# A four-layer hybrid decoder step on one core: turning and gating a head's output one block at a time between parts of the next head

## The reference

```python
out   = inner @ v + (q @ state) * cross_decay        # inner: masked q k^T
state = decay * state + (k * k_decay)^T @ v
# after the last chunk, per token and head:
o = (o - mu) * rsqrt(var + LN_EPS) * gn_g            # retention
o = o * rsqrt(mean(o * o) + LN_EPS) * rms_g          # GLA
y = (silu(g) * o) @ w_out
```

## Time and profile before

| | |
|---|---|
| median of 3 runs | 4918.33 us (4916.63 to 4928.33) |
| the profiled execution: its time | 4917.5 us |
| the profiled execution: its span | 4915.8 us |
| TensorE, VectorE, ScalarE busy | 95%, 66%, 45% of the span |
| mean granted TensorE clock | 0.967 |
| retention's recurrence | 1327.4 to 1468.2 us |
| GLA's recurrence | 2690.5 to 2777.2 us |

### The profile page before, as it was taken

One profiled execution on the slowest core, in us unless ns is written; L12 is line 12 of the kernel. 1 busy time (PEld: TensorE's weight loads), 2 busy tenths in 40 slices (PEclk: granted clock), 3 DMA queues, 4 the chain that ended last, 5 costly groups with the idle time before them and its releaser, 6 DMA issues. The chain is left out here.

```text
span 4915.8 us, 114294 instructions
## 1 busy us (share of the span) xinstructions
PE 4672.5 (95%) x49481; PEld 3647.5 (74%) x49481; DVE 3222.5 (66%) x6336; ACT 2203.9 (45%) x3067; POOL 739.9 (15%) x354
## 2 busy tenths in 40 slices
PE   7999999999969999999995799999999999999998
PEld 4677789995527777799964467778997667778997
DVE  3695778546355967686445487677845488677844
ACT  3675343444215763434442277433343377433343
POOL 0462000004002630000010056000001056000000
PEclk9999999999989999999997799999999899999999
DMA  3344444444363444444441344444444344444443
GB/s 121 120 162 159 146 151 145 156 164 162 135 234 118 168 159 147 153 146 152 160 144 32 105 144 159 155 148 150 147 160 139 111 140 159 156 148 150 147 160 125
DMA packets 286871, 717.26 MB, mean 146 GB/s; under 512 B 25795, under 2 KB 103444, under 8 KB 285348
## 3 DMA queue, kind: packets, MB, share of 16 engines
q1 hardware_dynamic: 286374, 709.95, 43.7%
HBM read 679.19 MB, written 30.67 MB: 144 GB/s over the span
## 5 line engine op out<-in xcount | busy, mean ns | idle before, releaser
L1698 DVE SCALAR_TENSOR_TENSOR b_lo<-raw,b_hi 128x1024 f16<-128x1024 f32 x800 | 980.1, 1225 | 894.3 <-ACT b_hi L1507 889.0
L1507 ACT ACTIVATE b_hi<-raw 128x1024 f16<-128x1024 f32 x800 | 842.9, 1054 | 1028.4 <-PE ps L1620 1028.4
L1599 PE MATMUL ps<-x_hi,b_hi 128*128 128x320 f16 x4608 | 1272.8, 300 | 23.9 <-DVE x_lo L253 23.6
L1600 PE MATMUL ps<-x_lo,b_hi 128*128 128x320 f16 x4608 | 1273.4, 300 | 0.0
L1617 PE MATMUL ps<-w_hi,b_lo 128*128 128x256 f16 x4096 | 1118.2, 273 | 0.0
L1617 PE MATMUL ps<-w_lo,b_hi 128*128 128x256 f16 x4096 | 1118.0, 273 | 0.0
L1617 PE MATMUL ps<-w_hi,b_hi 128*128 128x256 f16 x4096 | 1117.7, 273 | 0.0
L1620 PE MATMUL ps<-w_lo,b_hi 128*128 128x64 f16 x4096 | 789.3, 193 | 0.0
L1620 PE MATMUL ps<-w_hi,b_lo 128*128 128x64 f16 x4096 | 789.3, 193 | 0.0
L1620 PE MATMUL ps<-w_hi,b_hi 128*128 128x64 f16 x4096 | 789.0, 193 | 0.0
L1587 POOL TENSOR_TENSOR b_lo<-raw,b_hi 128x1024 f16<-128x1024 f32 x288 | 616.5, 2141 | 852.8 <-ACT b_hi L1505 852.8
(11 more groups left out here) (282 smaller groups left out, 6910.8 us busy)
## 6 DMA issues: line engine op xcount, KB each, us to landing
raw<-in_peer_uT SPq DMA_DIRECT2D x512, 512.0 KB, 3.3
raw<-in_peer_v SPq DMA_DIRECT2D x512, 512.0 KB, 3.3
raw<-in_peer_w_q SPq DMA_DIRECT2D x64, 512.0 KB, 4.0
w_in<-in_ret_w_in SPq DMA_DIRECT2D x48, 512.0 KB, 5.2
w_in<-in_sgu_w_in SPq DMA_DIRECT2D x32, 512.0 KB, 8.1
s_in<-in_state_ret SPq DMA_DIRECT2D x32, 512.0 KB, 6.5
out<-s_new SPq DMA_DIRECT2D x32, 512.0 KB, 4.4
w_in<-in_gla_w_in SPq DMA_DIRECT2D x24, 512.0 KB, 4.7
```

Source lines behind the costliest of these rows:

```text
L1507: nc.scalar.activation(b_hi[:, p], raw[:, p], ACT.Copy, scale=scale_of(n)).then_inc(s.hi, 1)
L1599: nc.tensor.matmul(dst, b_hi[:, p, k, :], x_hi[:, k, :], start=(k == 0), stop=False)
L1600: nc.tensor.matmul(dst, b_hi[:, p, k, :], x_lo[:, k, :], start=False, stop=False)
L1698: nc.vector.scalar_tensor_tensor(out=b_lo[:, p].rearrange("p k e -> p (k e)"), in0=raw[:, p].rearrange("p k e -> p (k e)"), scalar=scale_o ...
```

## The change

`turn` and `gate` take a block `f`. While head h runs, block 0 of head h-1 is turned after the updates of the prompt's first chunk, block 1 after `from_states(h, 0)`, block 2 (retention only) after the first half of the last updates, block 3 after the second half. VectorE gates blocks 0 and 1 after the states of chunks 0 and 1, and blocks 2 and 3 after each half of the last sample states. The products of scores and values no longer come after the whole turning: each waits only for ScalarE's reading of its own bank, and ScalarE reads in the same order (2, 0, 1). VectorE takes the reciprocal after the first of four updates. For the last head the blocks are turned into banks 7, 0, 1 and 2 with no wait between them.

```diff
+ORDER = (2, 0, 1)
+        def turn_bank(h, f):
+            return (TP, 0, 1, 2)[f] if h == H - 1 else TP
+                def turn(h, f):
+                    if h < 0 or f >= et:
+                        return
+                    n = h * et + f
                     pe.wait_ge(s.norm, 3 * (h + 1))
+                    if n and turn_bank(h, f) == TP:
+                        pe.wait_ge(s.tp_used, n)
...
                     for u in mine[:4]:
                         update(u)
-                    if h:
-                        turn(h - 1)
-                    for i in (2, 0, 1):
+                    for m, i in enumerate(ORDER):
+                        if h:
+                            pe.wait_ge(s.norm, 3 * (h - 1) + m + 1)
                         nc.tensor.matmul(ps[:, i, 0:width], att[:, h, i, :], v[:, i, ve], start=True,
                                          stop=False, skip_group_check=True)
...
                     for k in range(kd):
                         update((h, "p", 0, k))
+                    turn(h - 1, 0)
                     from_states(h, 0)
+                    turn(h - 1, 1)
...
-                    for u in mine[-4 * kd:]:
+                    for u in mine[-4 * kd:-2 * kd]:
                         update(u)
+                    turn(h - 1, 2)
+                    for u in mine[-2 * kd:]:
+                        update(u)
+                    turn(h - 1, 3)
                     from_states(h, 1)
-                turn(H - 1)
+                for f in range(et):
+                    turn(H - 1, f)
...
                     mine = units_of(h)
-                    for u in mine[:4]:
-                        state(u)
+                    state(mine[0])
                     if h:
                         factors(h - 1)
-                        gate(h - 1)
-                    for u in mine[4:]:
+                    for u in mine[1:4 * kd]:
                         state(u)
+                    for c in range(nchunk):
+                        for k in range(kd):
+                            state((h, "p", c, k))
+                        if c < 2:
+                            gate(h - 1, c)
+                    for u in mine[-4 * kd:-2 * kd]:
+                        state(u)
+                    gate(h - 1, 2)
+                    for u in mine[-2 * kd:]:
+                        state(u)
+                    gate(h - 1, 3)
                     moments(h)
...
-                    for i in range(3):
+                    for i in ORDER:
                         nc.scalar.activation(o_n[:, i, :], ps[:, i, 0:width], ACT.Identity, scale=rs[:, h, i:i + 1],
```

More of the change, by code:

```diff
@@ L689, in recurrent @@
         S0, S1 = state_slots(kd), 4
-        KV, TP = (3, 4, 5, 6), (7,)
+        KV, TP = (3, 4, 5, 6), 7
+        def turn_bank(h, f):
+            return (TP, 0, 1, 2)[f] if h == H - 1 else TP
         def units_of(h):
@@ L765, in update @@
                     nc.tensor.matmul(ps[:, KV[n % 4], 0:width], lhs, rhs, start=True, stop=True).then_inc(s.kv, 1)
-                def turn(h):
+                def turn(h, f):
+                    if h < 0 or f >= et:
+                        return
+                    n = h * et + f
                     pe.wait_ge(s.norm, 3 * (h + 1))
[L769 to L772, removed]
-                        for i in range(3):
-                            last = nc.tensor.transpose(ps[:, TP[0], 128 * i:128 * i + 128],
-                                                       o_n[:, i, 128 * f:128 * f + 128], ident[:])
-                        last.then_inc(s.tp, 1)
+                    if n and turn_bank(h, f) == TP:
+                        pe.wait_ge(s.tp_used, n)
+                    for i in range(3):
+                        last = nc.tensor.transpose(ps[:, turn_bank(h, f), 128 * i:128 * i + 128],
+                                                   o_n[:, i, 128 * f:128 * f + 128], ident[:])
+                    last.then_inc(s.tp, 1)
                 def from_states(h, g):
@@ L867, in factors, with gate @@
                     ins.then_inc(s.rs, 1)
[L869 to L882, removed]
+                def gate(h, f):
+                    if h < 0 or f >= et:
+                        return
+                    n = h * et + f
+                    dve.wait_ge(s.tp, n + 1)
+                    turned = ps[:, turn_bank(h, f), 0:384]
+                    nc.vector.scalar_tensor_tensor(out=gate_T[:, n, 0:PROMPT], in0=turned[:, 0:PROMPT],
+                                                   scalar=gain[:, n:n + 1], in1=gate_T[:, n, 0:PROMPT],
+                                                   op0=ALU.mult, op1=ALU.mult)
+                    for g in range(2):
+                        dst = gate_T[:, n, PROMPT + 32 * g:PROMPT + 32 * g + 32].rearrange("p (j t) -> p j t", t=LS)
+                        src = turned[:, PROMPT:384].rearrange("p (j r) -> p j r", j=4)[:, :, LS * g:LS * g + LS]
+                        last = nc.vector.scalar_tensor_tensor(out=dst, in0=src, scalar=gain[:, n:n + 1], in1=dst,
+                                                              op0=ALU.mult, op1=ALU.mult)
+                    last.then_inc(s.tp_used, 1)
@@ L893, in _ @@
+                    for u in mine[-4 * kd:-2 * kd]:
[4 more added lines that the diff above has]
+                    gate(h - 1, 3)
                     moments(h)
                 factors(H - 1)
-                gate(H - 1)
+                for f in range(et):
+                    gate(H - 1, f)
             @block.scalar
```

## The result

The changed kernel takes 4887.8 us (median of 4 runs, 4886.2 to 4895.0), the kernel before 4922.2 beside it; the ratio is 0.9936, 95% interval 0.9924 to 0.9949, a gain of 25 to 37 us. 4893 was forecast. The profiled execution took 4895.0 us with a span of 4893.3, so the two profiles that can be compared stretch by stretch differ by 22.5 us.

What follows compares the result with a forecast made beforehand. TensorE was taken to bound the kernel as a whole, but to wait in the stretches changed. Retention's 19.7 us and GLA's 5.0 sum to 24.7 off 4917.5, giving 4893; own range 4886 to 4900, with both clock rivals 4878 to 4907.

Steps and rivals of the forecast that it cites:

- Reciprocal: Retention boundary: reciprocal stands behind one state instead of four, so it starts earlier; gain 2.0 us.
- Products: Retention boundary: products of scores and values start 0.85 us after ScalarE instead of 8.25; gain 7.4 us.
- End: Last head: four turns into four banks need not wait for gates; gain 2.9 us in retention, 1.0 in GLA.
- GLA's boundary at 1.2 GHz: Between GLA heads: earlier reciprocal 1.1 and products 3.2, less 1.4 for turns and gate; gain 2.9 us a boundary.
- Gates in retention: Turns and gates in their new places delay VectorE's end and the next variances; cost 2.3 us a boundary.
- Clock in retention: Boundary between retention heads: between 1.3 us gained and 3.1 lost through TensorE's clock; a loss of 1.5 taken.
- second rival: Clock falls in retention's last updates, stays low into next head; GLA without fast head; gain 11.3 us, 4906, chance 0.20.
- Clock in GLA: GLA heads: one fast head instead of two, as turns ahead of the products are gone; 4.7 us lost.
- gaps alone: Retention boundary: if long idle gaps alone lose the clock, the shorter pause keeps it: gain 1.3 instead of loss 1.5.

Runs made afterwards that it cites:

- version with the pause filled: Changed kernel plus two unused products in TensorE's pause ahead of each later head's products of scores and values: median 4875.8 us, ratio 0.9898.
- second profile of the same program: The changed kernel profiled and timed once more, no edit: median 4894.2 us, ratio 0.9946.
- old order with its pause filled: Kernel before plus unused products in TensorE's pause ahead of the turns, six per boundary in retention, four in GLA: 4923.2 us, ratio 0.9997.
- the end alone: Kernel before with only the last head's blocks turned into four banks: median 4922.5 us, ratio 1.0002.

## Why the prediction was right

The forecast of 4893 us holds in its sum and in its terms for the order of work. Its terms for the clock were right in size in retention, partly by luck, and wrong in GLA.

Reciprocal, 2.0 us: 1.98 in the timeline, and 2.0 as an edit of its own. Products, 7.4 us: 7.42. End, 2.9 and 1.0: 3.3 and 1.1, the same with that edit alone; the gates of retention's last head follow each other at 0.71 us, not 0.84. GLA's boundary at 1.2 GHz, 2.9: 23.29 (at 0.53) to 20.47 (at 0.50), 2.8.

Gates in retention, a cost of 2.3 us: too high. The version with the pause filled has a period with no clock lost. Its stretch from the updates behind the products to the next variances, below the same stretch before:

```profile
1403.90:1420.65 16.75, 16.75 (x71) 5.78 (x72) 10.96 (x17) 0.00 (x0) 0.00 (x0) 1.00 0.76 280
1385.09:1403.28 18.19, 18.18 (x83) 7.31 (x84) 13.53 (x29) 0.00 (x0) 0.00 (x0) 1.00 0.90 339
```

The cost is 1.4. A gate between other work costs VectorE 0.71 us, not 0.84 (the earlier trace rows had it followed by a wait), and turn 3 with `from_states` stays hidden only while the clock is up. The rest of its period, 17.48 to 7.06, is shorter by 10.4 = 2.0 + 7.4 + 1.0 for faster products. 10.4 - 1.4 = 9.0, which is 34.2 to 25.25.

Clock in retention, a loss of 1.5 us: the mean period is 27.68 us against 25.25 without loss, 2.4 lost; the kernel before lost 1.0 in its products. That is 1.4 more, the forecast size. The place was half right. The loss at the pause was forecast; it came at two of three boundaries, and with the two added products at none. A second place is L790 at the head's end. The second rival (0.20) had a fall of the clock there and priced the products of states at 0.6 us; they cost 1.4 in two of three periods, since VectorE was done sooner than forecast and hid less. So 28.00 us is a loss at the pause alone, 26.68 one at L790 alone, and 28.35 has both. The mean is therefore luck in part: the second profile of the same program lost 1.9, not 2.4. As they are, 2.0 + 7.4 - 1.4 - 1.4 = 6.6 a boundary, 19.7 in three, where 16.8 was forecast.

Clock in GLA: one fast head expected of the four, one found, but it was the first, which the change does not touch. All three changed periods stayed at 1.2 GHz and gained nothing on their faster counterparts: the order of work gave 8.4 there and the clock took it all, where 4.7 was forecast. That the turns ahead of the products had helped to bring the clock back was argued; the experiments only show that denser work does it (e.g. 14.20 us at 1.00).

So the close sum is luck in part. In the stretches that the change touches, retention won 23.0 us where 19.7 was forecast and GLA 1.0 where 5.0 was; the two errors nearly cancel. GLA's total did fall by 5.0, but 4.0 of it is the unchanged first head, and retention's first head lost as much.

The timed gain, 31 us by the first ratio and 27 by the second, lies above the 24.7 of the sum; the second's interval takes it in. In the profile the recurrences gave 23.9 and the span 22.5. Runs of one kernel spread by 5 to 25 us, which is about the change itself; which stretch the unprofiled runs win is open. DMA did not decide: a period of 25.25 us moved 336 GB/s, more than the 313 of a longer one, although the share was near 1.0 at 26.7.

## What to carry to other kernels

Where a long step alternates between two engines, look first at what is queued behind it on each: here moving it off the path and cutting it into pieces gave 7.4 us a boundary for 1.4, and without the cutting a third of the timed gain was left. Price a stage at each level of TensorE's clock, read the mean clock beside every length, and do not believe a difference of some microseconds until the same code has been profiled twice. When a forecast meets the time, compare it stretch by stretch as well: here two errors of 3 to 4 us cancelled. A pause of TensorE that cannot be removed can be worth filling with products that nobody reads. Full-height ones in the pause paid here, small ones between narrow updates cost 8 us in the first head alone, and in the old order the filling gave nothing, so it must be measured in the kernel as it stands.

## What the runs showed of the hardware

The granted clock fell to 1.2 GHz near 1389.2 us of the old order with its pause filled, while the profile shows TensorE busy without a gap from 1378 to 1395.9; the work around the fall is 32-row updates and 32-column products. The Trainium skill ("TensorE: Matmul & The Clock Gate", section "HAM oscillation — how this bites in real kernels") warns of idle gaps; here the profile has none between the products, though their weight loads wait 2.6 us for VectorE between 1385.6 and 1389.2. Nor did the length of a pause decide: between the retention heads of the changed kernel's two profiles the clock was lost at pauses of 2.00, 2.44 and 2.44 us and kept at 2.43, 2.61 and 2.62. By gaps alone, which the prediction set beside its sum, the shorter pause keeps the clock; it did in three of six.

GLA's recurrence, whose TensorE is busy 86% of a period, stayed at 1.2 GHz for all three changed periods. With two products added per boundary it rose to 2.4 in the first and was there for all of the last.

At 2.4 GHz four 32-row updates of 512 columns take 1.99 us in a row, and one takes 1.05 when a full-height product stands before and behind it. Three fp32 transposes of 128 by 128 take 0.90 us at 1.2 GHz and 0.49 to 0.55 at 2.4.

A version may win its timeline terms and lose them in the same profile: the end alone (4.4 us read, ratio 1.0002) did.
